# The value pages of a decoder layer's paged attention: loaded and used one whole sample later, in another spacing

## The chip, the cores and the metric

One core of one Trainium2 chip runs the whole program. The metric is the device time of one execution, in microseconds (us), from its first to its last work on the device. The kernel before took 1707.8 us (median of 3 runs, 1703.45 to 1707.88).

## What is computed

One inference step of a layer, all in float32. 256 prompt tokens and 8 sample tokens (one new token for each of 8 samples, each with 2048 tokens in a paged cache) go through it together, as 264 columns.

```python
z = x @ w_in                      # 2048 -> 8192: q, k, v, u and the two gates
q, k, v, u, gate_a, gate_s = ...
attn = rms_norm(diff_attention(q, k, v), subln_g) * 0.8
ssm  = s5_branch(u)               # scan over 64 groups, GELU, GLU with w_glu
merged = gate_a * (attn @ w_proj_attn) + gate_s * (ssm @ w_proj_ssm)
h = layer_norm(alpha * x + merged @ w_out)
y = layer_norm(alpha * h + conv_ffn(h))
# diff_attention: softmax(map 0) - lam * softmax(map 1), 8 heads of 128 values
# a sample's keys and values: k_past = cache_k[page_table], 16 pages of 128 tokens
```

A page is 128 tokens by 1024 float32: 512 KB of keys and 512 KB of values. The 8 samples have 128 pages of each, together 134 MB of the 393 MB that the kernel moves.

## The kernel before, in words

**Engines.** TensorE (PE) multiplies; ScalarE (ACT) copies results out of PSUM, takes exponentials and issues the loads of the w_in and w_glu weights; VectorE (DVE) does the scans, the softmax steps and the sums of the sample scores; GpSimd (POOL) multiplies key pages by the query; SyncE (SP) issues all other loads and stores, in one fixed order. Every engine goes through a list written out by hand and waits for counters.

**The rounds.** The input projection and w_glu are cut into 72 tiles of 128 outputs. After the first 19 tiles comes a loop over `i` from 0 to 6, called rounds here. Round i has the tiles v(i+1), u(i+2) and four gates g, 24 steps of four matmuls (16 k-tiles to a tile, four steps to a tile); round 6 has no u and so 20 steps. `z_groups` runs the tiles, and a dictionary `at` (line 980 and on) gives the steps behind which other work is put in: the prompt's attention for head i (`scores`, `p_diff_rows`, `prompt_pv`), the state-space layer (`outputs_and_inputs`), and the samples' attention. Behind the loop, the tail runs g28 and g29, the eight half-deep glu tiles in pairs, and g30 and g31 (the last gate pair). Then come the two branch projections (`proj`), whose first matmul is line 1075.

**A sample's attention.** In round i the keys of sample i+1 come in, POOL multiplies half pages by the query (line 640), DVE sums them (`reduce_page`, line 1786), 16 pages to a round. In the next round the scores are shifted and exponentiated. Then `page_pv` (line 712) multiplies the probabilities by a value page: four matmuls of 16 x 256 added into PSUM bank 5, over the 16 pages. `copy_sums` (ACT) takes the sum out, `map_weights` (DVE) makes the weights of the two maps from the denominators, and `combine` (PE, line 901) puts them together; `combined` (ACT) copies the result. In round i, before, the pages 12 to 15 of sample i-1 are used behind steps 2 and 5, and the pages 0 to 11 of sample i, in pairs, behind steps 10, 12, 15, 17, 20 and 23.

**The buffers and SP's order.** The value pages have a ring of four buffers, the keys one of eight half pages. SP issues them from one list:

```python
def load_keys(b, p):                       # K4..K15 of sample i+1, N0..N3 of sample i+2
    for e in range(2):
        wait(sp, k_free, 2 * n + e - 7)    # the half page eight before it has been summed by DVE
def load_values(b, p):                     # V and P
    wait(sp, v_used, PAGES * b + p - 3)    # the page four before it has been used by PE
```

A wait of SP holds all that is behind it in the list. DVE sums page 5 of sample i+1 inside `states(t, 2)`, which needs what PE computes behind step 8; it sums page 7 behind `maxima(i, 0)`, which needs the scores behind step 12 (`scores(i, 0, 1)`); pages 8 to 11 follow on that. In the rounds with a u tile, POOL makes `fractions(4 * i + 8)` before page 8, and these need ACT's `turns`, which stand behind ACT's copy of the first gate tile (behind step 14).

**The end of the tail.** DVE scales and splits the prompt's attention (lines 1919 to 1926), makes the glu branch (1931 to 1933), and last the samples' part (1936 to 1926 again), for which PE, ACT and DVE go back and forth: `combine(7)` behind step 5 of the last gate pair, ACT's square (1483), PE's mean (1065), ACT's root (1487). PE's `proj` waits for all of them.

## Time and profile before

| | us |
|---|---|
| median of 3 runs | 1707.8 (1703.45 to 1707.88) |
| the profiled execution, its own time | 1714.25 |
| its span, first to last instruction | 1712.4 |
| PE busy in it | 1651.8 (96%) |
| DVE busy | 1128.6 (66%) |
| ACT busy | 648.8 (38%) |
| POOL busy | 389.3 (23%) |

The times of the trace are counted from the span's start. "Idle before" is time in which an engine had nothing to run, with what ended it. PE is busy nearly all the time, so an idle stretch of PE, or a stretch in which its clock is lower, is what can be won or lost. The rounds 0 to 6 lie at 174 to 630 us, the tail at 630 to 720 us; projections and the feed-forward part follow. A float32 matmul stands in the trace as two records, so that a step of four is a row "x8", and a value page is "x8" of line 712.

### The profile page before, as it was taken

What the parts mean: (1) busy time and instruction counts of PE and PEld (TensorE: products, weight loads), DVE (VectorE), ACT (ScalarE), POOL (GpSimd) and SP (SyncE); (2) the same over time, 40 slices, a digit from 0 to 9 for tenths busy, and PEclk for the clock granted to TensorE, in tenths of its full rate; (3) what the DMA queues carried; (4) which work ended last, traced back from release to release, by engine and by line L of the source; (5) the groups of instructions that cost most, each with busy time, mean ns of one, the idle gap of its engine ahead of it and who ended that gap; (6) DMA issues with size and microseconds to landing.
All of it is one profiled execution on the core that took longest, in us unless ns stands there. A gap on an engine that the chain in (4) does not pass through costs nothing. (4 is left out here: it accounts for less than half of the span.)

```text
span 1712.4 us, 31617 instructions
## 1 busy us (share of the span) xinstructions
PE 1651.8 (96%) x11730; PEld 1469.0 (86%) x11730; DVE 1128.6 (66%) x1748; ACT 648.8 (38%) x979; POOL 389.3 (23%) x341
## 2 busy tenths in 40 slices
PE   9999999989999999999997999999999999999997
PEld 7878766766766677699997999999999999999996
DVE  2373787887887753677666767777777776545545
ACT  2121343333443402333336544444444444333333
POOL 1057486586685740000001000000000000000001
PEclk9999999999999989999998999999999999999998
DMA  9699799999999987676663666667666575766651
GB/s 248 153 293 324 260 356 370 376 338 378 379 358 357 347 300 243 187 195 173 184 185 99 173 183 185 176 172 195 176 191 174 156 211 146 193 185 184 179 156 52
DMA packets 503778, 393.40 MB, mean 230 GB/s; under 512 B 25486, under 2 KB 451363, under 8 KB 503652
## 3 DMA queue, kind: packets, MB, share of 16 engines
q1 hardware_dynamic: 420724, 324.84, 63.0%
q10 hardware_dynamic: 82944, 67.11, 12.5%
q8 instruction: 67, 1.10, 0.3%
q14 instruction: 43, 0.35, 0.1%
HBM read 385.24 MB, written 7.02 MB: 229 GB/s over the span
## 5 line engine op out<-in xcount | busy, mean ns | idle before, releaser
L732 PE MATMUL bank<-work,weight_ring 128*128 128x264 f32 x2176 | 521.9, 395 | 2.4 <-DMA weight_ring<-in_w_in 1.9
L1479 ACT ACTIVATE weights_hi<-weight_ring 128x2048 fp32r<-128x2048 f32 (+1 forms) x166 | 309.8, 1866 | 514.3 <-PE bank L1076 389.7
L732 PEld LDWEIGHTS bank<-work,weight_ring 128*128 128x128 f32 x2176 | 409.8, 193 | 94.5 <-issue 24.3
L1949 DVE TENSOR_TENSOR weights_lo<-weight_ring,weights_hi 128x2048 fp32r<-128x2048 f32 (+1 forms) x166 | 369.0, 2224 | 112.3 <-ACT weights_hi L1479 67.5
L640 POOL TENSOR_TENSOR work<-work 128x512 f32<-128x512 f32 x256 | 318.4, 1277 | 65.8 <-DMA work<-in_cache_k 43.8
L1075 PE MATMUL bank<-h_hi,weights_hi 128*128 128x264 f32 x1344 | 330.9, 284 | 0.0
L1076 PE MATMUL bank<-h_lo,weights_hi 128*128 128x264 f32 x1344 | 330.1, 284 | 0.0
L1075 PEld LDWEIGHTS bank<-h_hi,weights_hi 128*128 128x128 f32 x1344 | 253.2, 188 | 0.0
L1076 PEld LDWEIGHTS bank<-h_lo,weights_hi 128*128 128x128 f32 x1344 | 252.7, 188 | 0.0
L670 POOL TENSOR_TENSOR work<-work,ffn_scratch 128x1056 f32<-128x1056 f32 x4 | 9.5, 2406 | 1059.7 <-ACT ffn_scratch L1197 1059.7
L1786 DVE TENSOR_REDUCE work<-work 128x8 f32<-128x512 f32 x256 | 165.2, 677 | 57.6 <-POOL work L640 57.2
L1081 PE MATMUL bank<-h_hi,weights_lo 128*128 128x264 f32 x1344 | 176.6, 284 | 0.0
L1075 PE MATMUL bank<-hidden_hi,weights_hi 128*128 128x264 f32 x688 | 169.7, 285 | 1.8 <-DVE ffn_scratch L2077 1.8
L1076 PE MATMUL bank<-hidden_lo,weights_hi 128*128 128x264 f32 x688 | 169.3, 284 | 0.0
L1081 PEld LDWEIGHTS bank<-h_hi,weights_lo 128*128 128x128 f32 x1344 | 168.4, 188 | 0.0
L1197 ACT ACTIVATE work<-bank 128x264 f32<-128x264 f32 (+9 forms) x117 | 40.2, 353 | 271.9 <-PE bank L681 101.3
L1075 PEld LDWEIGHTS bank<-hidden_hi,weights_hi 128*128 128x128 f32 x688 | 129.5, 188 | 2.1 <-DVE ffn_scratch L2077 2.0
L1076 PEld LDWEIGHTS bank<-hidden_lo,weights_hi 128*128 128x128 f32 x688 | 129.4, 188 | 0.0
L2074 DVE SCALAR_TENSOR_TENSOR ffn_scratch<-bank,conv_and_ln_parameters,ffn_scratch 128x255 f32<-128x255 f32 x86 | 41.5, 483 | 126.2 <-ACT ffn_scratch L1197 126.2
L1081 PE MATMUL bank<-hidden_hi,weights_lo 128*128 128x264 f32 x688 | 91.3, 284 | 0.0
L712 PE MATMUL bank<-work 128*16 128x256 f32 x1024 | 70.4, 382 | 20.4 <-DMA work<-in_cache_v 19.7
L1081 PEld LDWEIGHTS bank<-hidden_hi,weights_lo 128*128 128x128 f32 x688 | 86.7, 188 | 0.0
(272 smaller groups left out, 1910.0 us busy)
## 6 DMA issues: line engine op xcount, KB each, us to landing
weight_ring<-in_w_up SPq DMA_DIRECT2D x86, 1024.0 KB, 5.6
work<-in_cache_k SPq DMA_DIRECT2D x256, 256.0 KB, 6.0
work<-in_cache_v SPq DMA_DIRECT2D x128, 512.0 KB, 6.2
weight_ring<-in_w_in ACTq DMA_DIRECT2D x60, 1024.0 KB, 12.0
weight_ring<-in_w_down SPq DMA_DIRECT2D x32, 1024.0 KB, 6.0
weight_ring<-in_w_out SPq DMA_DIRECT2D x16, 1024.0 KB, 6.0
weight_ring<-in_w_down SPq DMA_DIRECT2D x16, 704.0 KB, 4.8
weight_ring<-in_w_proj_attn SPq DMA_DIRECT2D x16, 512.0 KB, 4.2
```

The source lines that it names most:

```text
L640: pool.tensor_tensor(half_page(2 * n + e), half_page(2 * n + e), q_b[b % 2][:, e * 512:(e + 1) * 512], ALU.mult).then_inc(kq_ready, 1)
L670: pool.tensor_tensor(c3, c3, mean_y.unsqueeze(1).to_broadcast([P, 4, N]), ALU.subtract).then_inc(cent_ready, 1)
L712: last = pe.matmul(bank[5][32 * g:32 * g + 16, 0:2 * P], score[b % 3][:, p * 16:(p + 1) * 16], page(v_pages, n)[:, g * 2 * P:(g + 1) * 2 * ...
L732: last = pe.matmul(bank[(n + m) % 2][:, 0:N], chunk_weight(g, k - c * per, m), tiles[k], start=(k == 0), stop=(k == len(tiles) - 1))
L1075: pe.matmul(dst[:, 0:N], weight(w_hi, off, k0 + k), highs[k], start=start and k == 0, stop=False)
L1076: last = pe.matmul(dst[:, 0:N], weight(w_hi, off, k0 + k), lows[k], start=False, stop=False)
L1081: last = pe.matmul(dst[:, 0:N], weight(w_lo, off, k0 + k), highs[k], start=False, stop=stop and k == len(highs) - 1)
L1197: return act.activation(dst, src, ACT.Copy, scale=scale)
L1479: act.activation(w_hi[:, (j % 2) * KT * P:(j % 2) * KT * P + k_tiles * P].bitcast(F32R), slot3(j, 0, k_tiles).rearrange("p k m -> p (k m)" ...
L1786: dve.tensor_reduce(score[b % 3][:, p * 16 + 8 * e:p * 16 + 8 * e + 8], half_page(2 * n + e).rearrange("p (m d) -> p m d", d=HD), AX.X, AL ...
L1949: dve.tensor_tensor(w_lo[:, cols].bitcast(F32R), slot3(off % SLOTS, 0, k_tiles).rearrange("p k m -> p (k m)"), w_hi[:, cols], ALU.subtract ...
L2074: n1 = ch.did(dve.scalar_tensor_tensor(y[:, 1:T], ps[:, 0:T - 1], par(1), y[:, 1:T], ALU.mult, ALU.add))
```

## The change

The value pages of sample i-1 are used in round i, all 16 of them, two pages behind each of the steps 2, 5, 8, 10, 14, 17, 20 and 23. In round 6, which has 20 steps, they stand behind steps 2, 4, 6, 8, 10, 12, 14 and 16, and pages 0 to 3 of sample 6 behind 18 and 20. Round 0 uses none. The other 28 pages are used in the tail. SP's list has the pages in the new order: each page from 4 to 15 one behind each key page. In the tail, the loads of the convolution's states and parameters now stand between the value pages 5 and 6 of sample 7. `combine` and `combined` come one round later, so the weights of the maps have two buffers. In the last gate pair, `combine(7)` moves from step 5 to step 1, the mean square of the samples from behind the pair to step 5, and the states' transposes to steps 6 and 7. ACT and DVE follow: the samples' part is put ahead of the glu branch in part, and DVE's wait for the stored outputs moves behind the first use of the two branches.

```diff
...
-    MAIL_ORDER += [("v_rows", _i), ("max_rows", _i), ("max", _i)] + ([("combine", _i - 1)] if _i else [])
+    MAIL_ORDER += [("v_rows", _i), ("max_rows", _i), ("max", _i)] + ([("combine", _i - 2)] if _i > 1 else [])
...
-MAIL_ORDER += [("attention", H - 1), ("kv_sample", 0), ("prompt_states", 0), ("sample_states", 0), ("combine", H - 1)]
+MAIL_ORDER += [("attention", H - 1), ("combine", H - 2), ("kv_sample", 0), ("combine", H - 1), ("prompt_states", 0), ("sample_states", 0)]
...
-                for what in ("K4", "Sk", "P14", "P15", "V0", "K5", "V1", "K6", "Sv", "V2", "K7", "V3", "K8", "Q", "V4", "K9",
-                             "V5", "K10", "V6", "K11", "V7", "V8", "K12", "V9", "K13", "V10", "K14", "V11", "K15", "V12",
-                             "N0", "N1", "V13", "N2", "N3"):
+                for what in ("K4", "Sk", "V4", "K5", "V5", "K6", "Sv", "V6", "K7", "V7", "K8", "Q", "V8", "K9", "V9", "K10", "V10",
+                             "K11", "V11", "K12", "V12", "K13", "V13", "K14", "V14", "K15", "V15", "N0", "N1", "F0", "F1",
+                             "N2", "N3", "F2", "F3"):
...
-                    elif kind == "V" and (i or p > 3):
+                    elif kind == "V" and i:
+                        load_values(i - 1, p)
+                    elif kind == "F" and i:
...
-                    elif kind == "P" and i:
-                        load_values(i - 1, p)
...
-            load_values(B - 2, 14)
-            load_values(B - 2, 15)
-            for p in range(3):
-                load_values(B - 1, p)
+            for p in range(4, 8):
+                load_values(B - 2, p)
...
-            for p in range(3, PAGES):
+            for p in range(8, PAGES):
+                load_values(B - 2, p)
+            for p in range(6):
...
+
+            for p in range(6, PAGES):
+                load_values(B - 1, p)
...
-                pages_pv(i, 2, 3)
...
-                if i:
-                    combine(i - 1)
+                if i > 1:
+                    combine(i - 2)
...
-                at = {2: lambda: (values_to_rows(i), pages_pv(i - 1, 12, 13)),
-                      3: lambda: max_rows(i),
-                      4: lambda: scores(i, 1, 1),
-                      5: lambda: (global_max(i), pages_pv(i - 1, 14, 15)),
-                      8: lambda: outputs_and_inputs(t, 0),
-                      10: lambda: (scores(i, 0, 0), pages_pv(i, 0, 1)),
-                      12: lambda: diagonal_scores_and_sums(i)}
+                at = {2: lambda: (values_to_rows(i), pages_pv(i - 1, 0, 1)),
+                      3: lambda: max_rows(i)}
...
-                    at |= {15: lambda: pages_pv(i, 4, 5),
-                           17: lambda: pages_pv(i, 6, 7),
-                           20: lambda: (pages_pv(i, 8, 9), outputs_and_inputs(t, 2)),
+                    at |= {4: lambda: scores(i, 1, 1),
+                           5: lambda: (global_max(i), pages_pv(i - 1, 2, 3)),
+                           8: lambda: (pages_pv(i - 1, 4, 5), outputs_and_inputs(t, 0)),
+                           10: lambda: (scores(i, 0, 0), pages_pv(i - 1, 6, 7)),
+                           12: lambda: diagonal_scores_and_sums(i),
+                           14: lambda: pages_pv(i - 1, 8, 9),
+                           17: lambda: pages_pv(i - 1, 10, 11),
+                           20: lambda: (pages_pv(i - 1, 12, 13), outputs_and_inputs(t, 2)),
...
-                           23: lambda: (pages_pv(i, 10, 11), keys_to_rows(i + 1))}
+                           23: lambda: (pages_pv(i - 1, 14, 15), keys_to_rows(i + 1))}
...
-                    at |= {14: lambda: pages_pv(i, 4, 5),
-                           16: lambda: (pages_pv(i, 6, 7), sample_bu()),
-                           18: lambda: pages_pv(i, 8, 9),
-                           20: lambda: (pages_pv(i, 10, 11), outputs_and_inputs(t, 2))}
+                    at |= {4: lambda: (scores(i, 1, 1), pages_pv(i - 1, 2, 3)),
+                           5: lambda: global_max(i),
+                           6: lambda: pages_pv(i - 1, 4, 5),
+                           8: lambda: (pages_pv(i - 1, 6, 7), outputs_and_inputs(t, 0)),
+                           10: lambda: (scores(i, 0, 0), pages_pv(i - 1, 8, 9)),
+                           12: lambda: (diagonal_scores_and_sums(i), pages_pv(i - 1, 10, 11)),
+                           14: lambda: pages_pv(i - 1, 12, 13),
+                           16: lambda: (pages_pv(i - 1, 14, 15), sample_bu()),
+                           18: lambda: pages_pv(i, 0, 1),
+                           20: lambda: (pages_pv(i, 2, 3), outputs_and_inputs(t, 2))}
...
-                     2: lambda: (values_to_rows(H - 1), pages_pv(B - 2, 12, 13)),
+                     2: lambda: (values_to_rows(H - 1), pages_pv(B - 2, 4, 5)),
...
-                     4: lambda: (scores(H - 1, 1, 1), pages_pv(B - 2, 14, 15)),
-                     6: lambda: global_max(B - 1)})
+                     4: lambda: (scores(H - 1, 1, 1), pages_pv(B - 2, 6, 7)),
+                     6: lambda: (global_max(B - 1), pages_pv(B - 2, 8, 9)),
+                     8: lambda: pages_pv(B - 2, 10, 11)})
...
-                    {4: lambda: (scores(H - 1, 0, 1), pages_pv(B - 1, 0, 1), combine(B - 2), denominators(B - 1)),
-                     8: lambda: pages_pv(B - 1, 2, 3)})
+                    {4: lambda: (scores(H - 1, 0, 1), pages_pv(B - 2, 12, 13), combine(B - 3), denominators(B - 1)),
+                     8: lambda: pages_pv(B - 2, 14, 15)})
...
-                    {4: lambda: (pages_pv(B - 1, 4, 5), p_diff_rows(H - 1)),
-                     8: lambda: pages_pv(B - 1, 6, 7)})
+                    {4: lambda: (pages_pv(B - 1, 0, 1), p_diff_rows(H - 1)),
+                     8: lambda: pages_pv(B - 1, 2, 3, 4, 5)})
...
-                    {4: lambda: pages_pv(B - 1, 8, 9), 8: lambda: pages_pv(B - 1, 10, 11)})
+                    {4: lambda: (pages_pv(B - 1, 6, 7), combine(B - 2)), 8: lambda: pages_pv(B - 1, 8, 9, 10, 11)})
...
+            def sample_mean_square():
+                pe.wait_ge(sq_ready, 2)
+                pe.matmul(bank[5][:, 0:H * B], v_mean_w[:, :], sq_sample, start=True, stop=True).then_inc(ms_done, 1)
...
-                    {2: states_out, 4: sample_states_out, 5: lambda: combine(B - 1)})
-            pe.wait_ge(sq_ready, 2)
-            pe.matmul(bank[5][:, 0:H * B], v_mean_w[:, :], sq_sample, start=True, stop=True).then_inc(ms_done, 1)
+                    {1: lambda: combine(B - 1), 5: sample_mean_square, 6: states_out, 7: sample_states_out})
...
-            pe.wait_ge(z_read, PROJ0)
+            pe.wait_ge(z_read, PROJ0 - 1)
+            pe.wait_ge(mail_read, len(MAIL_ORDER))
...
+                    if j == 1:
+                        pe.wait_ge(z_read, PROJ0)
...
+                if i > 1:
+                    copy_sums(i - 2)
...
-                if i:
-                    copy_sums(i - 1)
...
-                if i:
-                    combined(i - 1)
+                if i > 1:
+                    combined(i - 2)
...
+                if not whole:
+                    copy_sums(i - 1)
...
-            copy_sums(B - 2)
...
-            combined(B - 2)
+            combined(B - 3)
...
+            copy_sums(B - 2)
...
+            combined(B - 2)
...
+            combined(B - 1)
+            act.wait_ge(w_ready, B + 1)
+            act.activation(sq_sample.rearrange("p (h b) -> p h b", h=H), att3[:, :, T:N], ACT.Square).then_inc(sq_ready, 1)
+            act.wait_ge(ms_done, 5)
+            act.activation(root_sample, bank[5][:, 0:H * B], ACT.Sqrt, bias=small[:, 5:6]).then_inc(root_ready, 1)
...
-            take(("sample_states", 0))
-            copy(xs_rows, bank[2][:, :]).then_inc(mail_read, 1)
-            combined(B - 1)
...
-            act.wait_ge(w_ready, B + 1)
-            act.activation(sq_sample.rearrange("p (h b) -> p h b", h=H), att3[:, :, T:N], ACT.Square).then_inc(sq_ready, 1)
...
+            take(("sample_states", 0))
+            copy(xs_rows, bank[2][:, :]).then_inc(mail_read, 1)
...
-            act.wait_ge(ms_done, 5)
-            act.activation(root_sample, bank[5][:, 0:H * B], ACT.Sqrt, bias=small[:, 5:6]).then_inc(root_ready, 1)
...
-                wait(dve, mail, MAIL["combine", b - 1] + 1 if b else 0)
+                wait(dve, mail, MAIL["combine", b - 2] + 1 if b > 1 else 0)
...
+            dve.wait_ge(mail_read, MAIL["combine", B - 1] + 1)
+            dve.tensor_tensor(att3[:, :, T:N], att3[:, :, T:N], new_part, ALU.add).then_inc(w_ready, 1)
...
-            dve.wait_ge(mail_read, MAIL["combine", B - 1] + 1)
-            dve.tensor_tensor(att3[:, :, T:N], att3[:, :, T:N], new_part, ALU.add).then_inc(w_ready, 1)
...
-            dve.wait_ge(out_stored, 9 * 16)
...
+                    if j == 0:
+                        dve.wait_ge(out_stored, 9 * 16)
...
```

**The order on PE in round 6** (line 712 before, 715 after is a value page pair; 732 and 735 the tiles, x4 to a step; 850 and 853 the scores; 888 and 891 the maximum; 835, 838 and 824, 827 the state-space layer; 901, 904 `combine`; 893, 896 the denominators). Before, from step 5 to step 14:

```order
308 L888 MATMUL bank<-small,ones 128x16
309 L712 MATMUL bank<-work 16x256 x8
310 L732 MATMUL bank<-work,weight_ring 128x264 x12
311 L835 MATMUL bank<-conv_and_ln_parameters,work 32x256 x4
312 L824 MATMUL bank<-work 128x256 x4
313 L732 MATMUL bank<-work,weight_ring 128x264 x8
314 L850 MATMUL bank<-work 128x128
315 L712 MATMUL bank<-work 16x256 x8
316 L732 MATMUL bank<-work,weight_ring 128x264 x8
317 L712 MATMUL bank<-work 16x256 x8
318 L850 MATMUL bank<-work 128x128
```

And in the change, from step 5 on:

```order
300 L891 MATMUL bank<-small,ones 128x16
301 L735 MATMUL bank<-work,weight_ring 128x264 x4
302 L715 MATMUL bank<-work 16x256 x8
303 L735 MATMUL bank<-work,weight_ring 128x264 x8
304 L715 MATMUL bank<-work 16x256 x8
305 L838 MATMUL bank<-conv_and_ln_parameters,work 32x256 x4
306 L827 MATMUL bank<-work 128x256 x4
307 L735 MATMUL bank<-work,weight_ring 128x264 x8
308 L853 MATMUL bank<-work 128x128
309 L715 MATMUL bank<-work 16x256 x8
310 L735 MATMUL bank<-work,weight_ring 128x264 x8
311 L853 MATMUL bank<-work 128x128
```

The pages stand behind every second step, a pair is now ahead of the state-space layer's outputs of step 8, and the pair of step 12 is behind that step's scores, where before it was ahead of them.

**The order on PE in the last gate pair.** Before, from the transposes ahead of it to the first branch projection:

```order
375 L681 MATMUL bank<-ident,work 64x128 x2
376 L732 MATMUL bank<-work,weight_ring 128x264 x8
377 L681 MATMUL bank<-ident,work 32x128 x2
378 L732 MATMUL bank<-work,weight_ring 128x264 x8
379 L681 MATMUL bank<-ident,work 128x128 x4
380 L732 MATMUL bank<-work,weight_ring 128x264 x4
381 L901 MATMUL bank<-small,work 128x4 x2
382 L732 MATMUL bank<-work,weight_ring 128x264 x12
383 L1065 MATMUL bank<-work,v_mean_w 128x64
384 L1075 MATMUL bank<-att_hi,weights_hi 128x264
```

And in the change:

```order
372 L684 MATMUL bank<-ident,work 64x128 x2
373 L735 MATMUL bank<-work,weight_ring 128x264 x4
374 L904 MATMUL bank<-small,work 128x4 x2
375 L735 MATMUL bank<-work,weight_ring 128x264 x16
376 L1073 MATMUL bank<-work,v_mean_w 128x64
377 L735 MATMUL bank<-work,weight_ring 128x264 x4
378 L684 MATMUL bank<-ident,work 32x128 x2
379 L735 MATMUL bank<-work,weight_ring 128x264 x4
380 L684 MATMUL bank<-ident,work 128x128 x4
381 L735 MATMUL bank<-work,weight_ring 128x264 x4
382 L1086 MATMUL bank<-att_hi,weights_hi 128x264
```

`combine` and the mean square have steps of the tiles behind them now, and the states' transposes are at the end.

## Rows read from the trace of the kernel before

**Rows 1.** The page's part 1: busy us, share of the span, instructions

```profile
PE 1651.8 (96%) x11730; PEld 1469.0 (86%) x11730; DVE 1128.6 (66%) x1748; ACT 648.8 (38%) x979; POOL 389.3 (23%) x341
```

**Rows 2.** Waits of PE, whole span: us in total, times, longest us

```profile
PE bank L712 <- DMA work<-in_cache_v: 19.7, 16, 2.5
PE bank L1075 <- DVE att_lo L1926: 4.2, 1, 4.2
```

**Rows 3.** Waits of PE, window 240 to 565 us (rounds 1 to 5)

```profile
PE bank L712 <- DMA work<-in_cache_v: 16.3, 12, 2.5
```

**Rows 4.** Windows: us, busy of PE, PEld, DVE, ACT, POOL, PEclk, DMA share, GB/s

```profile
205.40:601.00 395.60, 375.45 (x2282) 267.19 (x2281) 312.46 (x513) 156.59 (x332) 283.23 (x242) 0.99 1.02 361
```

**Rows 5.** Waits of SP's DMA queue, window 187 to 660 us

```profile
SPq L443 <- PE bank L712: 81.0, 20, 12.2
```

**Rows 6.** Timeline of SP, round 2: start us, us, what, count

```profile
346.34 1.87 SPq L452 DMA_DIRECT2D work<-in_cache_k  x2
...
351.97 0.34 SPq L444 DMA_DIRECT2D work<-in_cache_v  x1
```

**Rows 7.** Timeline of ACT, POOL and PE, round 2, steps 14 and 20

```profile
341.20 0.39 ACT L1233 ACTIVATE work<-bank 128x264 f32<-128x264 f32 x1 [2.15 <-PE bank L732]
...
344.17 7.42 POOL L640 TENSOR_TENSOR work<-work 128x512 f32<-128x512 f32 x6
...
354.15 0.62 PE L712 MATMUL bank<-work 128*16 128x256 f32 x8
357.01 0.62 PE L712 MATMUL bank<-work 128*16 128x256 f32 x8 [2.24 <-DMA work<-in_cache_v]
```

**Rows 8.** The page's part 6: count, KB each, median us to landing

```profile
work<-in_cache_v SPq DMA_DIRECT2D x128, 512.0 KB, 6.2
```

**Rows 9.** Timeline of SP and PE, round 5, around step 20

```profile
550.61 0.34 SPq L444 DMA_DIRECT2D work<-in_cache_v  x1
...
552.86 0.62 PE L712 MATMUL bank<-work 128*16 128x256 f32 x8
```

**Rows 10.** Windows: slow clock after a wait, and none after another

```profile
252.70:256.10 3.40, 3.40 (x9) 2.62 (x8) 3.33 (x6) 2.00 (x4) 1.88 (x3) 0.50 1.03 368
357.00:360.50 3.50, 3.49 (x26) 2.40 (x27) 2.27 (x5) 0.00 (x0) 3.50 (x4) 1.00 1.04 394
```

**Rows 11.** Timeline of PE and SP, round 6, steps 8 to 14

```profile
587.00 1.06 PE L835 MATMUL bank<-conv_and_ln_parameters,work 128*32 128x256 f32 x8
...
589.07 3.83 PE L732 MATMUL bank<-work,weight_ring 128*128 128x264 f32 x16
...
599.67 0.49 PE L850 MATMUL bank<-work 64*128 64x128 f32 x2
...
586.80 0.35 SPq L444 DMA_DIRECT2D work<-in_cache_v  x1
```

**Rows 12.** Timeline of DVE, round 6: the sums of key pages 5, 7, 9 and 11

```profile
592.59 1.25 DVE L1786 TENSOR_REDUCE work<-work 128x8 f32<-128x512 f32 x2
...
600.99 1.27 DVE L1786 TENSOR_REDUCE work<-work 128x8 f32<-128x512 f32 x2
...
609.83 1.27 DVE L1786 TENSOR_REDUCE work<-work 128x8 f32<-128x512 f32 x2
...
615.92 1.27 DVE L1786 TENSOR_REDUCE work<-work 128x8 f32<-128x512 f32 x2
```

**Rows 13.** Waits of PE, window 565 to 640 us (round 6)

```profile
PE bank L712 <- DMA work<-in_cache_v: 3.1, 3, 2.0
```

**Rows 14.** Timeline of SP, DVE and PE in the tail and at its end

```profile
690.68 0.43 SPq L513 DMA_DIRECT2D work<-in_state_conv  x1
...
695.78 0.42 SPq L520 DMA_DIRECT2D work<-in_ln_b  x1
...
715.93 2.36 DVE L1933 TENSOR_TENSOR ssm_lo<-work,ssm_hi 128x2112 fp32r<-128x2112 f32 x1
...
723.97 0.56 PE L1075 MATMUL bank<-att_hi,weights_hi 128*128 128x264 f32 x1 [4.24 <-DVE att_lo L1926]
```

More of the change, by code:

```diff
@@ L898, in combine @@
                 pe.wait_ge(w_ready, b + 1)
-                w_map = small[:, 576:584].rearrange("p (g e) -> p e g", e=2)
+                w_map = small[:, 576 + 8 * (b % 2):584 + 8 * (b % 2)].rearrange("p (g e) -> p e g", e=2)
                 for e in range(2):
@@ L1818, in map_weights @@
                 dve.wait_ge(mail_read, MAIL["sums", b] + 1)
-                wait(dve, mail, MAIL["combine", b - 1] + 1 if b else 0)
+                wait(dve, mail, MAIL["combine", b - 2] + 1 if b > 1 else 0)
                 link(dve.reciprocal(small[:, 560:576], sums[:, 32 * b + 16:32 * b + 32]))
                 link(dve.tensor_tensor(small[:, 560:576], small[:, 560:576], signs, ALU.mult))
-                dve.tensor_reduce(small[:, 576:584], small[:, 560:576].rearrange("p (h j) -> p h j", j=2), AX.X,
+                dve.tensor_reduce(small[:, 576 + 8 * (b % 2):584 + 8 * (b % 2)], small[:, 560:576].rearrange("p (h j) -> p h j", j=2), AX.X,
                                   ALU.add).then_inc(w_ready, 1)
```

## Prediction

> **What bounds the kernel now.** I read the page first: PE is busy for 96% of the span [rows 1], so only its idle time, its clock and its own work can move the end. The waits of PE come next: matmuls of a value page waited 19.7 us for their page in 16 waits, and the first branch projection 4.2 us for the samples' attention [rows 2]. That is what this change can win. Its number of matmuls stays: 11730 records, the 128 value pages are only used elsewhere. 16.3 us of the 19.7 lie in rounds 1 to 5 [rows 3], 3.1 in round 6 [rows 13], the last 0.3 in round 0.
>
> Third, why is a page late? Over the six stretches from round 0's denominators to round 6's the DMA engines are full (share 1.02, 361 GB/s, [rows 4]), but SP's own queue stood for 81.0 us waiting for a value page's buffer [rows 5]. So order counts as well as bandwidth. The timeline of round 2 shows how. ACT copies the first gate tile at 341.20, behind step 14; with that POOL gets its fractions and goes on with key page 8 at 344.17 [rows 7]. SP may load key page 12 only when page 8 has been summed, so K12 goes out at 346.34, though its list had stood there before, and the value pages behind it go out later still: the one behind K13 at 351.97 [rows 6]. Step 20 is reached at 354.15, and its second page is 2.24 us late [rows 7]. What sets a page's issue is the key page ahead of it in SP's list, and that hangs on PE's own progress.
>
> **Rounds 1 to 5.** The change takes pages 14 and 15 away from the place behind K4, where they were late. But pages 12 and 13 are now used behind step 20, and stand in the list behind K12 and K13. The steps up to 14 have as many pages ahead of them as before (four pairs), and from 14 to 20 two pairs as before, so the distances of rows 6 and 7 hold: page 13 takes the place that page 10 has now. It goes out 2.2 us ahead of step 20 (351.97 against 354.15; in round 5 550.61 against 552.86, [rows 6, 7, 9]) and needs 6.2 us to land, the median of the value pages [rows 8]. It is needed 0.5 us into the step, behind page 12. Wait: 6.2 - 2.2 - 0.5 = 3.5 us, in each of five rounds 17.5 us, in place of 16.3. With transfers as short as they may get when PE stands (I take 4 us) it is 6.5, with 8 us 26.5. Sum: +1.2 us, bounds -10 and +10. Round 0 uses no pages: -0.3 us. Its 12 pages less are 12 more later, so nothing.
>
> **The clock.** Behind the longest of these waits, 2.5 us in round 1 [rows 2], PE had 3.4 us at half its clock (0.50, the lower level of 1.2 GHz); behind the 2.24 us of round 2 it kept the upper one [rows 7, 10]. A slow stretch costs half of 3.4, 1.7 us. The 0.99 over the rounds [rows 4] is two such stretches in rounds 1 to 5. Waits of 3.5 us in one piece are nearer to the 4.24 us at the end, which also was followed by a slow stretch, than to 2.24. I take four for the five rounds: two more, +3.4 us, with 0 and +5 as bounds. The Trainium skill says in "TensorE: Matmul & The Clock Gate", section "HAM oscillation", that a DMA wait between bursts of matmuls throttles PE again; applied to every wait it would give all five rounds and every wait below, some 9 us more than I take. The row behind the 2.24 us wait shows full clock, so I go by the rows.
>
> **Round 6** is where I see most. It has 20 steps for 16 pages, a pair behind every second step, and the same SP list: each page from 4 on behind its key page. Here the lock closes. Steps of PE are 1.92 us (3.83 for two, [rows 11]).
> Step 8 needs page 7, which takes the place of the V issued at 586.80, lands at 593.0, and is needed at 587.9 (587.00 today, 0.65 of the 3.1 us of waits ahead gone, one more pair of 1.06 us ahead, 0.5 for page 6): 5.1 us. This pair now stands ahead of step 8's state-space outputs, so these start at 593.5 instead of 587.00 and DVE's sum of key page 5 ends at 600.3 instead of 593.84 [rows 11, 12].
> Step 10 needs page 9, behind K9, which needs that sum: issue 601.6 (1.3 us after the sum, as two half pages go out in between), landed 607.8, needed 600.4: 7.4 us.
> Step 12 needs page 11, behind K11, which needs the sum of key page 7, which needs the scores of the same step. Scores end at 612.6; the sum ends 2.1 to 2.6 us after (600.16 to 602.26 today); issue 616.5, landed 622.7, needed 614.1: 8.6 us. This wait can't vanish whatever the bandwidth is: it is asked for in the hook that comes before it.
> Step 14 needs page 13, behind K13; the sum of page 9 ends 8.8 us after that of page 7 (611.10 against 602.26): issue 625.3, landed 631.5, needed 627.5: 4.0 us. Step 16 needs page 15, sum of page 11 14.9 us after that of page 7: 1.3 us.
> Together 26.4 us, less today's 3.1 [rows 13]: +23.3 us. Landing 3 us sooner takes 15 off, landing 2.5 us later adds 12. Three of the five waits with a slow stretch: +5.1 (0 to 8.5).
>
> **The tail** has 28 pages for 20, paid for in round 0. In glu 2 and 3 four pages (2 to 5) stand behind step 8 with four buffers: page 4 may load when page 0 has been used, four half steps earlier. From there 0.5 + 0.4 + 3.8 + 1.1 = 5.9 us to its use, and 0.8 + 6.2 to its landing; with page 5 1.9 us. Behind page 5 SP now issues the states and parameters, 5.5 us (690.68 to 696.20, [rows 14]), before page 6: 2.2 us. Pages 10 and 11 the same once more: 1.7. Sum +5.8 and one slow stretch, 1.7: +7.5 (0 to 15).
>
> **The end.** The samples' root is taken while DVE still does the glu branch, which ended at 718.29 [rows 14]. Then 1.5 us of small steps are left, so PE starts at about 720.2 instead of 723.97, 0.5 us after its last tile: -3.7, and without its slow stretch -1.7: -5.4 us. Between 0 and -5.9. DVE's wait for the stores moves behind the first products; 5 us of matmuls cover it.
>
> **Sum:** -0.3 + 1.2 + 3.4 + 23.3 + 5.1 + 7.5 - 5.4 = +34.8 us on the profiled execution of 1714.25 us (span 1712.4 and 1.85 around it): 1749.1. That execution is 6.45 us over the median of 1707.8; on the median the sum gives **1742.6 us**.
>
> **Rivals.**
> A. *The even spread works, and the waits go.* If the lock on the key pages were slack, every page would be four buffers and some 13 us ahead. The waits of 16.3 + 3.1 + 0.3 us go, with them two slow stretches in rounds 1 to 5 (3.4), and 5.4 at the end: -28.5 us, 1679; with the tail's waits 1687. For it: pages 14 and 15 are now the latest, up to 2.49 us, and lose their bad place. Against: rows 6 and 7, where K12 leaves only 5 us after step 14. It decides if page 13 lands within 2.7 us of its issue, where the median is 6.2 [rows 8]. Chance 0.10.
> B. *Bandwidth binds in the rounds.* The engines' share is 1.02 [rows 4], and five rounds have the same bytes as before. Then waits move but keep their sum, round 6 has less to load and costs only half, +11; with tail and end +13: 1721. The Trainium skill gives in "DMA: Bandwidth & Descriptors", section "Where 436 GB/s comes from", some 358 GB/s for what one core gets from HBM; the trace has 361 over six rounds, so by that rule no order of loads makes a full round shorter, and A is barred. Chance 0.17.
> C. *Nothing to be measured*: waits of round 6 are met by faster landings (3 us), rounds 1 to 5 gain their lower bound, the end its 5.4. 23.3 - 15 - 10 - 5.4 + 7.5: 0. Chance 0.05.
> D. *The lock costs more*: landings of 8 us and slow clock after each wait: +34.8 + 9 + 12 + 6 = +62, 1770. Chance 0.13.
>
> **Numbers.** My forecast, 0.55: 1742.6, its own range 1727 to 1757. B and D lie beside it; two in ten are left out, at A's end and beyond D's middle: 1708 to 1766. A measurement of this kernel can tell 0.3% (5 us) from no change. Faster 0.11 (A and a little of C), same 0.05, slower 0.84.
>
> **What would show it.** Right: waits for value pages of 40 to 50 us in all, in round 6 alone over 20, the longest behind step 12; in each of rounds 1 to 5 one of 3 to 4 us at step 20 and none behind step 5; slow clock stretches in most of them; the wait for att_lo under 1 us. The lock is wrong if PE's wait behind step 12 of round 6 is under 5 us. A is right if the waits on the value loads fall under 5 us in all. B is right if rounds 1 to 5 keep their 65.9 us each (395.6 / 6) with waits at other places. The end is wrong if the first branch projection still waits over 3 us.

## The result, and the profile after

The changed kernel took **1766.1 us** (median of 4 executions, 1762.2 to 1769.3) against 1707.8. The ratio on record is 1.0315, 95% interval 1.0272 to 1.0358 (the quotient of the two medians is 1.0341). One more execution of the kernel before, at 2346.5 us, is left out of its median. The change is slower, as forecast, but by 58 us where the forecast of 1742.6 had 35. The time lies outside the forecast's own range (1727 to 1757), at the upper end of the wider one (1708 to 1766), and next to rival D's 1770. The profiled execution took 1769.26 us, its span is 1767.5.

The page of the changed kernel, parts 1 and 6, to read beside [rows 1, 8]:

```profile
PE 1672.7 (95%) x11730; PEld 1480.0 (84%) x11730; DVE 1125.7 (64%) x1748; ACT 652.4 (37%) x981; POOL 389.4 (22%) x341
...
work<-in_cache_v SPq DMA_DIRECT2D x128, 512.0 KB, 7.0
```

Its waits of PE over the whole span (us in total, times, longest), beside [rows 2]:

```profile
PE bank L715 <- DMA work<-in_cache_v: 47.4, 26, 8.4
PE bank L735 <- DMA weight_ring<-in_w_in: 11.7, 1, 11.7
PE bank L891 <- DVE small L1821: 3.5, 1, 3.5
PE bank L1086 <- ACT work L1211: 0.5, 1, 0.5
```

Same matmuls; busy time is 20.9 us up, which is slow clock and no work. The waits for value pages went from 19.7 to 47.4 us. A wait in the start-up, for a piece of w_in, went from 1.9 to 11.7 us, and one of 3.5 us for a maximum in round 1 is new. The 4.2 us for att_lo are gone, 0.5 is left. The same by place, first 250 to 585 us (rounds 1 to 5, beside [rows 3]), then 585 to 665 (round 6, beside [rows 13]), then the tail, 722 to 745:

```profile
PE bank L715 <- DMA work<-in_cache_v: 20.8, 15, 2.6
...
PE bank L715 <- DMA work<-in_cache_v: 22.3, 7, 8.4
...
PE bank L715 <- DMA work<-in_cache_v: 4.3, 4, 1.7
```

SP's queue shows the lock by itself. How long it waited for DVE from 187 to 660 us, the window of [rows 5], before and after:

```profile
SPq L452 <- DVE work L1786: 68.8, 42, 7.5
...
SPq L452 <- DVE work L1804: 185.2, 79, 23.9
```

Line 452 is a key page's load, and what it waits for is DVE's sum of an earlier key page. SP's waits for a value page's buffer fell from 81.0 to 3.1 us: in the changed kernel SP stands almost only for DVE. (With the list of experiment 2 it still stands 116.3 us for DVE, and that does little harm, since the value pages are out ahead.)

To see where the time came from, cut both traces at the denominators' matmuls, one pair a round, and at the first branch projection. The rows of rounds 1, 5 and 7, before and then after:

```profile
272.81 0.41 PE L893 MATMUL bank<-work,ones 128*128 128x32 f32 x2 [0.27 <-ACT work L1197]
...
535.83 0.41 PE L893 MATMUL bank<-work,ones 128*128 128x32 f32 x2 [0.27 <-ACT work L1197]
...
663.90 0.41 PE L893 MATMUL bank<-work,ones 128*128 128x32 f32 x2 [0.27 <-ACT work L1197]
```

```profile
277.23 0.41 PE L896 MATMUL bank<-work,ones 128*128 128x32 f32 x2
...
552.83 0.41 PE L896 MATMUL bank<-work,ones 128*128 128x32 f32 x2 [0.27 <-ACT work L1211]
...
713.64 0.41 PE L896 MATMUL bank<-work,ones 128*128 128x32 f32 x2 [0.27 <-ACT work L1211]
...
780.34 0.36 PE L1086 MATMUL bank<-att_hi,weights_hi 128*128 128x264 f32 x1 [0.50 <-ACT work L1211]
```

Where pages moved from one stretch to another (0.53 us of matmuls each) that is taken out. "Again" is a second profile of the changed kernel (first experiment).

| stretch | before | after, again | pages moved | net, again | the prediction's terms |
|---|---|---|---|---|---|
| start to round 1 | 272.8 | 277.2, 270.4 | -12 | +10.8, +4.0 | -0.3 |
| round 1 to 5 | 263.0 | 275.6, 277.5 | 0 | +12.6, +14.5 | +4.6 |
| round 5 to 7 | 128.1 | 160.8, 160.4 | +8 | +28.5, +28.1 | +28.4 |
| round 7 to the projection | 60.1 | 66.7, 69.2 | +4 | +4.5, +7.0 | +7.5 - 3.7 |
| from there to the end | 988.4 | 987.2, 987.3 | 0 | -1.2, -1.1 | -1.7 |

The slow stretch of the clock at the end (-1.7) began with the projection, so it stands in the last row. The +4.6 is for five rounds, of which one has its step 20 in the row below; in the changed kernel that one wait is 2.2 us. Round 6 is where the prediction saw most, and there its sum stands. The miss is in the full rounds and ahead of them.

**Round 6, the lock at work.** Timelines of SP, PE, DVE and POOL of the changed kernel:

```profile
618.51 0.92 SPq L452 DMA_DIRECT2D work<-in_cache_k  x2
620.21 0.34 SPq L444 DMA_DIRECT2D work<-in_cache_v  x1
...
627.35 1.05 PE L715 MATMUL bank<-work 128*16 128x256 f32 x8 [8.40 <-DMA work<-in_cache_v]
...
634.18 0.48 PE L853 MATMUL bank<-work 64*128 64x128 f32 x2
...
634.70 0.42 DVE L1770 SCALAR_TENSOR_TENSOR work<-bank,work 128x256 f32<-128x256 f32 x1 [12.53 <-PE bank L853]
635.50 1.27 DVE L1804 TENSOR_REDUCE work<-work 128x8 f32<-128x512 f32 x2
...
636.35 0.92 SPq L452 DMA_DIRECT2D work<-in_cache_k  x2
638.04 0.34 SPq L444 DMA_DIRECT2D work<-in_cache_v  x1
...
643.89 1.05 PE L715 MATMUL bank<-work 128*16 128x256 f32 x8 [7.45 <-DMA work<-in_cache_v]
```

Value page 9 goes out at 620.21, right behind key page 9, and PE has stood for it since 618.95. So the scores of step 12 come at 634.18, DVE has waited 12.5 us for them, its sum at 635.50 sets key page 11 free, that goes out at 636.35 and value page 11 behind it at 638.04. PE needs that one at 636.44, ahead of its own issue. Each wait makes the next. The buffer of page 11 was free long before: its last reader, page 7, had ended at 612.3, 25.8 us ahead of the issue.

### The profile page after: what moved, and what is told of

It is laid out like the page before. It is cut to its first block and busy times, and to the rows that moved or that the text cites. A ratio compares the mean times of both kernels' runs of the same rounds, so it can differ in the third digit from the quotient of the medians.

```text
span 1767.5 us, 31626 instructions
## 1 busy us (share of the span) xinstructions
PE 1672.7 (95%) x11730; PEld 1480.0 (84%) x11730; DVE 1125.7 (64%) x1748; ACT 652.4 (37%) x981; POOL 389.4 (22%) x341
## 3 DMA queue, kind: packets, MB, share of 16 engines
q10 hardware_dynamic: 82944, 67.11, 12.5%
## 5 line engine op out<-in xcount | busy, mean ns | idle before, releaser
L735 PE MATMUL bank<-work,weight_ring 128*128 128x264 f32 x2176 | 536.0, 402 | 12.2 <-DMA weight_ring<-in_w_in 11.7
L735 PEld LDWEIGHTS bank<-work,weight_ring 128*128 128x128 f32 x2176 | 419.3, 197 | 111.0 <-issue 26.9
L1211 ACT ACTIVATE work<-bank 128x256 f32<-128x256 f32 (+8 forms) x117 | 40.3, 354 | 329.8 <-PE bank L684 112.4
L715 PE MATMUL bank<-work 128*16 128x256 f32 x1024 | 75.1, 400 | 47.4 <-DMA work<-in_cache_v 47.4
L715 PEld LDWEIGHTS bank<-work 128*16 128x16 f32 x1024 | 21.6, 96 | 84.1 <-DMA work<-in_cache_v 61.3
```

Of the source, the lines that this page charges most:

```text
L715: last = pe.matmul(bank[5][32 * g:32 * g + 16, 0:2 * P], score[b % 3][:, p * 16:(p + 1) * 16], page(v_pages, n)[:, g * 2 * P:(g + 1) * 2 * ...
L735: last = pe.matmul(bank[(n + m) % 2][:, 0:N], chunk_weight(g, k - c * per, m), tiles[k], start=(k == 0), stop=(k == len(tiles) - 1))
L1211: return act.activation(dst, src, ACT.Copy, scale=scale)
```

## The experiments

The kernel before was run beside each group, on whichever chip the group got: its medians were 1709.3 us (first four runs), 1716.5 (next four), 1710.4 (next three) and 1716.4 (last). So versions are compared by their ratio to it. These ratios are the recorded ones and not quotients of medians; where the two tell different things, both are given.

**1. The changed kernel again.**

> The changed kernel once more, unchanged. Both theories: 1766 us within 5, value waits of PE near 47 us, two of them over 7 us in round 6. What is open is the start-up: the first round's denominators came at 213.8 us instead of 205.4, with one wait of 11.7 us for a chunk of in_w_in near 80 us, whose load ACT issued just behind SP's store of the Toeplitz rows. If that is chance of the queues, this profile shows the wait gone or of another size in one execution in a few (then some 10 us of the loss are no property of the change); if it belongs to the program, the same 11 to 12 us stand there again.

1766.2 us, ratio 1.0346 (1.0312 to 1.0379). Round 6's two waits are 8.7 and 7.6 us. The start-up's wait is 5.3 us this time and round 0's denominators come at 202.9 instead of 213.8; yet the end comes only 2.8 us sooner, since the next rounds take part of it back. So the 11.7 us are no fixed property of the change.

**2. to 4. Values ahead of keys in SP's list**, in all rounds, in rounds 0 to 5 only, in round 6 only. The list of the full rounds, from its first entry on:

```diff
-"K4", "Sk", "V4", "K5", "V5", "K6", "Sv", "V6", "K7", "V7", "K8", "Q", "V8", "K9", "V9", "K10", "V10",
-"K11", "V11", "K12", "V12", "K13", "V13", "K14", "V14", "K15", "V15", ...
+"K4", "Sk", "V4", "V5", "K5", "V6", "K6", "Sv", "V7", "K7", "K8", "Q", "V8", "V9", "K9", "K10", "V10",
+"V11", "K11", "V12", "V13", "K12", "K13", "V14", "V15", "K14", "K15", ...
```

In round 6 (20 steps) the pairs from page 8 on stand one key page further ahead.

> Only SP's list is written in another order: each pair of value pages goes out ahead of the key page that stood ahead of it, in rounds 0 to 6. Lock theory: the pages were late since they stood behind key pages that wait for DVE's sums, so the value waits of PE fall from 47 to under 10 us, and the slow-clock stretches behind them go: rounds 1 to 5 get some 20 us of waits and 10 us of clock shorter, round 6 some 20 and 8, together 1766 - 55 = 1710 us (1695 to 1725). Rival, bandwidth: the engines are full in the rounds, so the key pages come late instead, DVE and the scores wait, rounds 1 to 5 keep their 69 us each and only round 6 gets some 10 us shorter: 1756 us.

> The same order for rounds 0 to 5 only; round 6 keeps each value page behind its key page. Lock theory: 20 us of waits and some 10 us of slow clock in rounds 1 to 5 go, 1766 - 30 = 1736 us; the two waits of 7 to 9 us in round 6 stay. Rival, bandwidth: rounds keep 69 us each, 1766 us.

> The value pages ahead of the key pages in round 6 only. Lock theory: the waits behind steps 10 and 12 of round 6 (8.4 and 7.5 us) fall under 2 us and two slow stretches go: 1766 - 20 - 8 = 1738 us; rounds 1 to 5 unchanged at 69 us. Rival, bandwidth: round 6 has 16 pages in 20 steps and can't be fed faster; the waits move to the key pages and the time stays within 8 us of 1766.

Measured: all rounds 1709.2 us, ratio 1.0003 (0.9978 to 1.0028); rounds 0 to 5 1728.6, 1.0144 (1.0093 to 1.0195); round 6 1746.1, 1.0196 (1.0130 to 1.0262). Off the 1.0346 beside them that is 3.4%, 2.0% and 1.5%, and the parts add up: the order of one list is worth the whole loss. The lock had 1710, 1736 and 1738 us for the three; round 6 alone gave less than that, and its four executions spread from 1728.5 to 1749.3. The windows of rounds 1 to 5 (us, busy of PE, PEld, DVE, ACT, POOL, PEclk, DMA share, GB/s), of the kernel before, the changed kernel, and the changed kernel with values ahead:

```profile
272.80:535.80 263.00, 249.49 (x1520) 177.79 (x1520) 208.57 (x341) 103.28 (x220) 187.06 (x160) 0.99 1.02 364
```

```profile
277.20:552.80 275.60, 256.33 (x1521) 180.39 (x1520) 207.31 (x342) 103.85 (x220) 187.31 (x160) 0.96 0.98 350
```

```profile
271.20:518.80 247.60, 245.88 (x1522) 177.93 (x1521) 206.12 (x343) 102.89 (x220) 187.50 (x160) 1.00 1.06 387
```

Three orders of the same loads and matmuls: 65.8, 68.9 and 61.9 us a round. At 61.9 PE is busy for 245.9 of 247.6 us at full clock. The share of 1.02 before did not mean that the engines could give no more: they gave 387 GB/s. Rival B is refuted, also by its own sign: in the changed kernel the rounds did not keep their time. The Trainium skill's 358 GB/s from HBM for one core, in "DMA: Bandwidth & Descriptors", section "Where 436 GB/s comes from", is no bound for this program: 387 over 248 us. (Right ahead of that section the page ties the figure to two cores streaming at once; here one runs.)

With round 6 alone reordered, its waits of 8.7 and 7.6 us become 2.8 and 3.5.

**5. The kernel before with the same idea.** Its steps stay, with pages used in their own round; SP's list follows the order in which buffers come free.

```diff
-"K4", "Sk", "P14", "P15", "V0", "K5", "V1", "K6", "Sv", "V2", "K7", "V3", "K8", "Q", "V4", "K9",
-"V5", "K10", "V6", "K11", "V7", "V8", "K12", "V9", "K13", "V10", "K14", "V11", "K15", "V12",
-"N0", "N1", "V13", "N2", "N3"
+"V0", "V1", "K4", "Sk", "K5", "V2", "K6", "V3", "Sv", "K7", "K8", "Q", "V4", "V5", "K9", "K10",
+"V6", "V7", "K11", "V8", "V9", "K12", "V10", "V11", "K13", "K14", "V12", "K15", "V13",
+"N0", "N1", "N2", "V14", "V15", "N3"
```

> The kernel before, with the steps of its value pages untouched; only SP's list is written in the order in which the buffers come free, so that pairs of value pages go out ahead of the key pages that wait for DVE's sums. Lock theory: the loss was never in where the pages are used but in what stands ahead of them, so the waits of 16.3 us in rounds 1 to 5 and 3.1 in round 6 go and their slow stretches with them, 1708 - 19 - 5 = 1684 us (1676 to 1692), rounds at 61.7 us each as in the changed kernel with this order. Rival, the spread is what pays: at the old steps (pairs at 2, 5, 10, 12, 15, 17, 20, 23, eight of them in 21 steps) the pages stay late with any order, 1700 us or more. Rival, bandwidth: 1708 us.

1694.0 us, ratio 0.9880 (0.9824 to 0.9936): some 21 us faster. Its waits for value pages between 215 and 620 us, in place of the 19.7 of [rows 2]:

```profile
PE bank L708 <- DMA work<-in_cache_v: 0.5, 1, 0.5
```

Each of the five stretches between the denominators of rounds 0 and 5 takes 61.8 us. With either set of steps the order decides, and a spread over the round buys nothing beyond it: the changed steps with their good order are at 1.0003, the old ones at 0.9880. By one profile of each, that difference does not lie in the full rounds. It is in the wait for the maximum (3.3 us, see below), and between the denominators of rounds 5 and 7 (137.5 us against 124.0, of which eight pages more are 4.2), and 3 us in the tail.

**6. The end alone, on the kernel before.** Only the part in the last gate pair, with its work on ACT and DVE:

```diff
-                    {2: states_out, 4: sample_states_out, 5: lambda: combine(B - 1)})
-            pe.wait_ge(sq_ready, 2)
...
+                    {1: lambda: combine(B - 1), 5: sample_mean_square, 6: states_out, 7: sample_states_out})
```

> The kernel before with the part of the change at the end alone: the last samples' attention is finished inside the last gate pair, its root taken there, DVE adds it ahead of the glu branch, and the wait for the stores stands behind the first products. By the term of the prediction: the wait of 4.2 us at the first branch projection falls to 0.5 and the slow stretch behind it goes, -5.4 us, 1702 us. Rival: DVE's glu branch now ends later by the adding that stands ahead of it, and PE waits for that as long as before: 1708 us.

1705.0 us, ratio 0.9967 (0.9932 to 1.0003), 5.6 us as expected, though the interval just holds no change (the medians are 11.5 us apart, so the size is loose). The row that answers to the last of [rows 14], with no slow stretch behind it:

```profile
713.73 0.36 PE L1077 MATMUL bank<-att_hi,weights_hi 128*128 128x264 f32 x1 [0.49 <-ACT work L1202]
```

**7. Two entries only.** In the changed kernel:

```diff
-"K12", "V12", "K13", "V13",
+"V12", "V13", "K12", "K13",
```

> The changed kernel; in SP's list two entries alone trade places: V12 and V13 stand ahead of K12 and K13 instead of each behind its own. The prediction's lock said just this: page 13 is late at step 20 since it stands behind K13, which waits for DVE's sum of key page 9. Then the waits at step 20 of rounds 1 to 5 (1.7 to 2.8 and 1.9 us, some 20 us in all) go, and with them their slow stretches (30 us at half clock, 15 us): 1766 - 35 = 1731 us, at least 1740. Round 6 as before at two waits of 7 to 9 us. Rival: the queue as a whole runs late and any page is, so that the waits turn up at steps 23 and 2 instead, and rounds stay over 67 us: 1755 us or more.

1744.2 us, ratio 1.0217 (1.0170 to 1.0265), 1.3% or 22 us less than the changed kernel. It lies between the two theories: the waits at step 20 are gone, and with them half of the sum of the rounds' waits; the other half stands mostly at step 23 (1.1 to 1.9 us in each round), where page 15 is late behind K15. A round takes 65.1 us in place of 68.9. SP and PE in round 3:

```profile
400.32 4.41 SPq L444 DMA_DIRECT2D work<-in_cache_v  x3
406.97 4.80 SPq L452 DMA_DIRECT2D work<-in_cache_k  x4
...
414.79 1.06 PE L715 MATMUL bank<-work 128*16 128x256 f32 x16
```

and the waits of 250 to 570 us:

```profile
PE bank L715 <- DMA work<-in_cache_v: 10.6, 10, 1.9
```

Pages 12 and 13 go out ahead of the key pages (x3 with page 11), and step 20 runs as x16 without a wait.

**8. The states' place in the tail.** Changed kernel, the loads of states and parameters behind page 15 instead of ahead of page 6.

> The changed kernel; the states and parameters are loaded behind value page 15 again, as in the kernel before, instead of ahead of page 6. The prediction priced their place in the tail at 2.2 us for page 6 and 1.7 for pages 10 and 11. By that the waits at pages 6 and 10 (1.7 and 1.6 us and their seconds of 0.4 and 0.7) fall to under 1 us each, 1766 - 4 to 6 = 1761 us. Rival: the four buffers alone make the pages late (8 pages behind two steps), the waits stay, and PE then also waits for the states behind the last pages: 1766 us or more.

One execution, 1761.7 us, which can't be told from the 1762.2 to 1769.3 of the changed kernel. The waits in the tail (715 to 735 us):

```profile
PE bank L713 <- DMA work<-in_cache_v: 3.5, 4, 1.7
```

They were 4.3. Page 6 goes out 0.8 us after its buffer is free, where it was 4.9, and is still 1.7 us late (it was 1.5), as it takes 8.1 us to land instead of 6.4. So the states' place costs less than 1 us of waits, where I had priced it at 2.2 and more. That the eight pages behind two steps make the rest is not shown: with two pages to a step (9) pages 6 and 7 are late as well, behind landings just as long.

**9. Spreading what was left.** On top of 2: round 6's pairs as soon as buffers are free, pages 2 and 3 ahead of N3, two pages at most behind a step of the tail, states behind page 11.

> The changed kernel with values ahead (1709 us), and three further edits: in round 6 every pair goes out as soon as its buffers are free (pages 10 and 11 ahead of key page 9, 14 and 15 ahead of key page 12), pages 2 and 3 ahead of the third half of the next keys, and in the tail two pages at most stand behind a step (4 and 5 behind step 1 of glu 4 and 5, 10 and 11 behind step 1 of glu 6 and 7), with the states and parameters loaded behind page 11. If the remaining waits are queue positions as the others were: round 6 loses some 6 of its 8 us of waits, the tail its 4.9, with three to four slow stretches: 1709 - 11 - 6 = 1692 us. Rival: in round 6 the loads are at the limit of the engines (16 pages in 20 steps, 24.9 MB in 71.5 us), only the tail's part comes, 1702 us.

1703.8 us, ratio 0.9936 (0.9903 to 0.9969), 0.67% or 11 us less than 2, give or take 7 by the two intervals. Waits for value pages after 550 us fall from 13.2 to 6.7 us. The time lies between the rival's 7 us and the 17 hoped for and rules out neither; the waits rule out that round 6 can't be fed faster (2.8 us there, where it was 8.8). 3.9 of the 6.7 are in the tail, at pages 6 and 7, which went out 0.8 and 1.5 us after their buffers were free and took 8.2 and 8.6 us to land.

**10. The start-up.** On top of 2, one line ahead of SP's store of the Toeplitz rows: `sp.wait_ge(z_read, 4)`.

> The changed kernel with values ahead (1709 us), and SP waits for ACT's fourth eviction ahead of its store of the Toeplitz rows. In the five profiles so far the store kept all later transfers for 30 us and more, and PE waited 1.9, 3.2 and 5.3 us where ACT's third load of in_w_in had been issued ahead of it, and 7.0, 10.6 and 11.7 us where it came behind. If this race is what makes the start-up 202 to 214 us long, the wait is at most 5 us in every execution and the median falls by half of the difference, 1709 - 4 = 1705 us, with less spread between executions. Rival: the keys behind the store come 4 us later and the first round starts later by as much: 1709 to 1713 us.

1706.8 us, ratio 0.9977 (0.9948 to 1.0005) against 1.0003: the intervals overlap, the gain of 4 us is not settled. PE's wait near 80 us was 5.6, put down to a copy of ACT. Over the 13 profiles with the whole store: where it came over 1 us ahead of ACT's third load (three of them), the wait was 10.6, 11.1 and 11.7 us; in all others the waits there sum to 1.9 to 7.0. The added line rules out the first kind, not the second, and the times still spread over 1702.9 to 1715.5.

**11. All that paid, on the kernel before:** the list of 5, the end of 6, the line of 10.

> The kernel before with three edits: SP's list in the order in which buffers come free (1694 us alone), the last gate pair's end of the change (the wait of 4.2 us at the first branch projection went in its own run), and SP's store of the Toeplitz rows behind ACT's fourth eviction. If they add up: 1694 - 5.4 - 2 = 1687 us, ratio to the kernel before 0.981 to 0.986. Rival: the end's gain was cover for something that is late anyway, or the store sent later delays the first keys: 1692 us or more.

**1684.5 us**, ratio **0.9849** (0.9818 to 0.9881), six executions within 5.3 us. It beats both kernels: by the ratios 1.5% under the one and 4.5 to 4.8% under the other. Its interval overlaps that of 5 alone, so what the other two edits add is not settled. Between 200 and 700 us PE waits for no value page.

**12. The store in two halves**, four heads behind ACT's fourth eviction, four behind its sixth.

> The fastest version so far (1684.5 us, six executions within 1682.3 to 1687.6), with SP's store of the Toeplitz rows in two halves of four heads, the first behind ACT's fourth eviction, the second behind its sixth. In eleven profiles the load of in_w_in behind the whole store took 26 to 32 us to land, and PE waited 1.9 to 11.7 us for one near 80 us. If the store's length in the queues makes that wait, the load between the halves lands in about half of that, the wait (5.9 us in the profile of the version) falls under 1.5 us and a slow stretch with it, 1684.5 - 6 = 1678 us. Rival: the queues hold the same bytes either way, a later load of in_w_in becomes the late one, and the keys start 3 us later: 1682 to 1688 us.

1716.7 us, ratio 1.0004 (0.9979 to 1.0030): it gives the whole gain away, and my theory of it was wrong. PE waited 26.9 us for one piece of w_in. Windows (columns as above) while the store runs, whole in the kernel before, then half in this one:

```profile
68.00:76.00 8.00, 6.10 (x29) 4.92 (x28) 0.69 (x1) 0.00 (x0) 0.00 (x0) 0.95 0.50 67
```

```profile
76.00:84.00 8.00, 8.00 (x45) 6.91 (x44) 2.95 (x5) 0.00 (x0) 0.00 (x0) 1.00 0.24 29
```

Eight heads keep half of the 16 engines busy at 67 GB/s, four heads a quarter at 29. Half the bytes on half the engines take as long as the whole, and there are two such stores: from the first issue to the load that waits for all of it (119.18) it is 67.1 us, where the kernel before had 37.1.

## Why the prediction was right, and where it was off

**The cause was right.** A value page is late since it stands in SP's list behind a key page that waits for DVE's sum, and that hangs on PE. Taking the place away took the loss away (2 to 5, 7); round 6's chain is in the trace. The direction follows from it.

**Round 6 was right in sum, and that is in part luck.** +28.4 was forecast, +28.5 and +28.1 measured. But the waits grew by 19.2 us (3.1 to 22.3) in place of 23.3, and the slow clock by 8.9 in place of 5.1. (Before, two slow stretches held 10.2 us of busy PE. After, five held 3.4, 5.3, 5.7, 10.2 and 3.4, of which half is lost.) The two misses cancel. Nor does it fit wait by wait: behind steps 8, 10, 12, 14 and 16 it gave 5.1, 7.4, 8.6, 4.0 and 1.3 us, the trace has 1.8, 8.4, 7.5, 0 and 2.5, and 2.2 us at pages 1 to 3 in front. Longest is the one behind step 10, not step 12.

**The waits of the full rounds were right** in size: 3.5 us forecast at each step 20, 17.5 in five; measured 3.9, 4.5, 3.5, 3.9 and 2.2, together 18.0. In round 3 page 13 went out at 429.57, 2.3 us ahead of the step, where 2.2 was forecast. The waits come in two pieces, since page 12 behind K12 is late as well. Other small ones bring the sum to 20.8.

**The clock of the full rounds is the step that failed.** I took four slow stretches in five rounds, and there are four behind the step-20 waits; but I took 3.4 us for the length of one, from [rows 10]. Three of the four are 6.8. The trace of before had shown that length too, in round 6, where I did not look:

```profile
614.50:621.30 6.80, 6.80 (x26) 6.18 (x26) 3.31 (x7) 0.00 (x0) 6.77 (x6) 0.50 0.94 370
```

These are the windows of the one in round 3 and of the longest in round 6, and the sum over the five slow stretches of rounds 1 to 5 (one stands behind the wait for the maximum):

```profile
434.60:441.40 6.80, 5.42 (x22) 3.07 (x23) 2.98 (x6) 0.00 (x0) 6.80 (x7) 0.50 0.84 313
659.90:670.10 10.20, 10.20 (x40) 9.27 (x40) 0.69 (x1) 0.07 (x1) 0.00 (x0) 0.50 0.32 118
...
sum 30.60, PE 24.21 PEld 12.76 DVE 14.13 ACT 3.27 POOL 30.28; mean PE 4.84 PEld 2.55 DVE 2.83 ACT 0.65 POOL 6.06
```

At 0.50, the level of 1.2 GHz, half of PE's busy part is lost: 5.4 us busy cost 2.7. The five lose 24.2 / 2 = 12.1 us, against 3.4 for the two before: +8.7 in place of +3.4. The same mis-sizing stands in round 6, as said. The Trainium skill tells in "TensorE: Matmul & The Clock Gate", section "HAM oscillation", of waits for a DMA of 3 to 5 us between bursts of matmuls, each of which throttles PE. The rows agree with it for four of the five rounds, with pairs of 3.5 to 4.5 us together. Shorter waits go either way: behind 0.24 and 1.91 us in round 5 the clock stayed up, behind a single 2.54 us in round 6 it fell.

**A wait that I did not see**: 3.5 us in round 1 for the global maximum, off DVE. It stands at 3.3 to 3.7 us in all nine profiles of kernels that use no value page in round 0, and is at most 0.7 in the five with the old steps. I had written that round 0's twelve pages less cost nothing. They gave DVE and POOL 6.4 us to finish the keys; PE now is there first. That this is the reason is read from these profiles, and no run changed it alone.

**The start-up** lies outside the change. It differs by up to 11 us between executions of one program.

**The tail** was right in sum in one profile (+4.5 measured against +3.8 with the end's wait in it: waits 4.3 where 5.8 was forecast, two slow stretches where one) and 3.2 us short in the other (+7.0). Its working was wrong: the states' place hardly counts (8). **The end** was right: 4.24 us fell to 0.50, and -5.4 was measured as -5.6 (6), within a wide interval.

Added up by the rows of the table, the profiles lie 20.4 and 17.7 us over the sum. 8.0 and 9.9 us of it are rounds 1 to 5, by the clock and the smaller waits (over all five rounds of the first profile 5.3 and 3.3 us, a little of it in the rows beside). 11.1 and 4.3 lie ahead of round 1's denominators: 3.5 and 3.6 are the wait for the maximum, a part is the slow stretch behind it, and the rest is start-up. The tail and the end have 1.2 and 3.8.

**Rival A** (waits go) fell with its own test, 47.4 us against 5. With another list its waits in the full rounds do go (0.5 us are left), but not its time: 1709 us, not 1679 to 1687. **Rival D** (the lock costs more) named nearly the right time, 1770, with landings of 8 us and slow clock behind each wait. The landings were 7.0 us in the median and the clock did not fall behind each wait, so of its two reasons the second is nearer, and its time is in part luck.

## What to carry to other kernels

Where one engine issues the loads of several streams in one list, each load waits for all that stands ahead of it. Write the list by the time at which each buffer comes free, and compare that with the issue in the timeline; here pages went out 10 to 26 us after their buffers were free, and they were late by their place, not by bandwidth. Look for a ring in such a list (load A behind load B, B released by work that waits for A), since there a wait feeds itself. And price a wait of the matmul engine with the slow clock behind it.

## What the runs showed of the hardware that was not expected

- A DMA share of 1.02 was no ceiling: 364 GB/s before, 387 with another order (share 1.06), for 248 us on end, and for 309 us in the version of 11.
- The number of DMA engines that a store uses followed the size of its outermost dimension: 8 heads a share of 0.50, 4 heads 0.24. The Trainium skill has the rule in "DMA: Bandwidth & Descriptors", section "Why a DMA increments its semaphore by 16 and not by 1": at most 16, and a divisor of that dimension on both sides of the transfer; the trace agrees. A load of w_in behind the half store took 47 us to land (64.5 to 111.6), where its like in the kernel before took 23.3.
- In the changed kernel's rounds a slow stretch of the clock lasted 3.4, 6.8 or 10.2 us, and not by the wait's length: 10.2 us behind 2.5 us of waiting, and 10.2 at a wait of 8.4, in which it began. What it costs is half of PE's busy part: 5.1 us in the one case, 2.6 in the other.
